# Suffix sums from a high and a low part, and steps of the second block moved up

## The chip, the core and the metric

The kernel is one program on one core of a Trainium2 chip. Its engines work side by side, each through its own list of instructions in order: TensorE (PE, the matrix products; its weight loads are listed apart as PEld), VectorE (DVE), ScalarE (ACT), GpSimd (POOL), and SyncE (SP), which here issues the transfers of weights. They meet at semaphores. The metric is the device time of one launch in microseconds (us), lower is better; it was 1090.6 us before the change, the median of 3 runs.

## The reference

Input is x of 256 tokens by 1024 features, all in float32. A first block of two layers (a mixer of mLSTM, block-sparse and native sparse attention, then a feed-forward part) is followed by a second block of two layers that mixes three kinds of attention. Cut to what matters here:

```python
def first_block(x, ...):
    for l in range(DEPTH):                                   # 2 layers
        h = rmsnorm(x, norm_mix[l])
        proj = jnp.einsum('bsd,de->bse', h, w_in[l])
        ...                                                  # y_m, y_b, y_n
        mix = jnp.concatenate([y_m, y_b, y_n], axis=-1)
        x = x + jnp.einsum('bse,ed->bsd', mix, w_out[l])
        h = rmsnorm(x, norm_ffn[l])
        u = jnp.square(jax.nn.relu(jnp.einsum('bsd,df->bsf', h, w_ff1[l])))
        x = x + jnp.einsum('bsf,fd->bsd', u, w_ff2[l])

def stick_breaking_attention(q, k, v):                       # 8 heads of 64
    for i in range(2):                                       # queries in blocks of 128
        z = jnp.einsum('bhqd,bhkd->bhqk', q[:, :, q0:q1], k[:, :, :q1]) * scale
        strict = pos[:q1][None, :] < pos[q0:q1][:, None]
        log_keep = jnp.where(strict, jax.nn.log_sigmoid(-z), 0.0)
        log_rest = lax.cumsum(log_keep, axis=3, reverse=True) - log_keep
        a = jnp.where(strict, jnp.exp(jax.nn.log_sigmoid(z) + log_rest), 0.0)
        outs.append(jnp.einsum('bhqk,bhkd->bhqd', a, v[:, :, :q1]))

def hybrid_layer(x, w_in, ..., w_out, g_pre, g_post, ...):   # second block, 2 layers
    h = rms_norm(x, g_pre)
    p = h @ w_in
    qa, ka, va, ga, qs, ks, vs, gs, qf, kf, vf, gf, ff = jnp.split(p, split_at, axis=-1)
    ya = diff_attention(qa, ka, va, ...) * jax.nn.silu(ga)
    yb = stick_breaking_attention(qs, ks, vs) * jax.nn.silu(gs)
    yc = forgetting_attention(qf, kf, vf, cum_log_f) * jax.nn.silu(gf)
    y = jnp.concatenate([ya, yb, yc], axis=-1) @ w_out
    return x + rms_norm(y, g_post)
```

The second block's output has the shape of x, and it is the only output.

## The kernel before

**Weights.** All weights are streamed from memory in units of 128 x 1024 float32 (512 KB). SyncE issues a unit's transfer into one of four `raw` slots. ScalarE rounds it to `w_hi` (L1405, type fp32r), VectorE takes the rest as `w_lo` (L1824), and a product of float32 accuracy is three fp32r matmuls, high by high, high by low, low by high (`exact_product`, L852 to L854; in the first feed-forward product, ff1, L918 and L920). Activations are kept in such parts too (`h_parts`, `mixT_hi`, `mixT_lo`). ScalarE and VectorE split weights ahead of need: before a step that reads a bank, `split_to` issues the splits of the units up to AHEAD = 3 in front of it. So a split stands in each engine's list between the other steps, and what stands behind it waits for it.

**Order.** One list of steps is written at the start by Python loops; each engine then issues its share in that order. In the second block `side2(p)` puts the attention's steps at position p, which is behind the p-th unit of the layer's projections. For a stick-breaking head the stages are Z (PE: scores; ScalarE: abs, exp, log of one plus it, L1669), K (VectorE, L2323: adds max(z, 0), so that `softp` holds the softplus of the score), R (PE, L1333 to L1335: suffix sums of `softp`, added to the scores that are still in the bank; ScalarE then takes the exponential) and V (PE: values). Heads go in pairs, four pairs a layer, every third position. `softp` is 128 x 384 for a head: queries 0 to 127 see 128 keys, queries 128 to 255 see 256.

**Suffix sums.** R multiplies by two constants of 128 x 128, a triangle (`C_RTRI`) and a matrix of one value (`C_NONES`). Both and `softp` are plain float32, which PE takes in two passes. The rest of the layer's PE work beside them is the projections, 256 columns at a time, and the heads' products.

**Gates and the mix.** `gate_silu` (ScalarE, L1650) takes the silu of the gates and loads that function's table for it and another one behind it. `mix_full` (VectorE, L2310) multiplies attention output in a bank by the gate, for four pairs of heads' columns n = 0 to 3; `mix_hi` (ScalarE) and `mix_lo` (VectorE, L2316) split the product. The forgetting heads ("fox") have the stages S (PE: scores; VectorE: row maxima, L1910 and L1913; ScalarE: exps, L1442 and L1444), N (VectorE: reciprocals of the sums, L1923 and L1924; GpSimd: scaling, L1720), T (PE: transposes, L1061, into bank 6; ScalarE: copy `probsT`, L1448) and V (PE: L1038, into bank 7).

**Banks.** PE's results go into eight banks of PSUM. `use(key, bank)` names the bank of a step; the PE opens it only when the reader of the bank's last content has freed it. The first feed-forward product has passes t = 0, 1, ...; each has four groups c of results, all in banks 4 to 7, which VectorE reduces (L2201) before the next pass opens them. The second feed-forward product (ff2) then opens banks 0 to 3 for four sums.

**Ends of the first block's layers.** The output projection ends in a "tail", whose last three features f = 1, 2, 3 wait for the transposed mix (`mix_turn`, two of them). Norm factors are a diagonal matrix (`factor_diag`, L1885), which a product (L1114) turns into a row.

## Time and profile before

| what | value |
| --- | --- |
| median of 3 runs | 1090.6 us (1089.24 to 1091.53) |
| profiled execution | 1088.39 us, its span 1086.6 us |
| granted TensorE clock, mean | 0.997 |
| PE busy | 1064.1 us, 98% of the span |
| DVE busy / ACT busy / POOL busy | 741.4 / 618.6 / 80.8 us |
| DMA | 179.04 MB, 165 GB/s mean |
| chain that ended last | PE 79%, DVE 8%, ACT 6%, issue 4%, DMA 3% |

All engines' times come from one profiled execution. Busy time counts an instruction from start to end; matmuls are pipelined, so a matmul's duration is longer than the distance to the next one's start, and that distance is what a matmul costs in a stream. "Idle before" is the time in which the engine had nothing in work ahead of an instruction, with what ended it.

### The profile page before, as it was taken

What the parts mean: (1) busy time and instruction counts of PE and PEld (TensorE: products, weight loads), DVE (VectorE), ACT (ScalarE), POOL (GpSimd) and SP (SyncE); (2) the same over time, 40 slices, a digit from 0 to 9 for tenths busy, and PEclk for the clock granted to TensorE, in tenths of its full rate; (3) what the DMA queues carried; (4) which work ended last, traced back from release to release, by engine and by line L of the source; (5) the groups of instructions that cost most, each with busy time, mean ns of one, the idle gap of its engine ahead of it and who ended that gap; (6) DMA issues with size and microseconds to landing.
All of it is one profiled execution on the core that took longest, in us unless ns stands there. A gap on an engine that the chain in (4) does not pass through costs nothing.

```text
span 1086.6 us, 16764 instructions
## 1 busy us (share of the span) xinstructions
PE 1064.1 (98%) x6396; PEld 908.1 (84%) x6396; DVE 741.4 (68%) x1296; ACT 618.6 (57%) x1039; POOL 80.8 (7%) x96
## 2 busy tenths in 40 slices
PE   8999999999999999999999999999999999999997
PEld 7898888888888988888888887898987778989876
DVE  5889777677667888787766675684465657844554
ACT  6776754344436768563444354855656548556562
POOL 1010110000000100110000000004011000040120
PEclk9999999999999999999999999999999999999999
DMA  9853365555657534446566654654444456544432
GB/s 320 268 153 118 99 189 182 190 173 187 211 183 216 168 112 133 123 151 208 162 207 198 191 160 147 197 156 136 120 150 136 136 156 194 156 131 123 155 118 76
DMA packets 89404, 179.04 MB, mean 165 GB/s; under 512 B 8989, under 2 KB 20637, under 8 KB 89325
## 3 DMA queue, kind: packets, MB, share of 16 engines
q1 hardware_dynamic: 88605, 176.58, 52.1%
q10 hardware_dynamic: 720, 1.40, 0.4%
q8 instruction: 51, 0.84, 0.3%
q14 instruction: 28, 0.23, 0.1%
HBM read 176.90 MB, written 1.05 MB: 164 GB/s over the span
## 4 chain that ended last, share of the span: by engine, by line
PE 79%; DVE 8%; ACT 6%; issue 4%; DMA 3%; SPq 0%; DVEq 0%; POOL 0%; ACTq 0%; POOLq 0%
PE bank L852 18%; PE bank L854 17%; PE bank L853 17%; PE bank L918 11%; PE bank L920 5%; DVE w_lo L1824 2%; DMA raw<-in_w_in 2%; PE bank L1004 2%; ACT w_hi L1405 2%; PE bank L953 2%; PE bank L1061 1%; PE bank L1038 1%; DVE vecs L1833 1%; PE bank L1027 1%; PE bank L1333 1%
## 5 line engine op out<-in xcount | busy, mean ns | idle before, releaser
L1824 DVE TENSOR_TENSOR w_lo<-raw,w_hi 128x1024 fp32r<-128x1024 f32 (+1 forms) x319 | 385.7, 1221 | 228.1 <-ACT w_hi L1405 225.4
L1405 ACT ACTIVATE w_hi<-raw 128x1024 fp32r<-128x1024 f32 (+1 forms) x319 | 330.7, 1052 | 181.9 <-PE bank L854 96.7
L918 PE MATMUL bank<-h_parts,w_hi 128*128 128x512 f32 x512 | 180.7, 396 | 1.0 <-DVE arena L2201 0.7
L852 PE MATMUL bank<-h_parts,w_hi 128*128 128x256 f32 x512 | 149.3, 292 | 0.0
L853 PE MATMUL bank<-h_parts,w_hi 128*128 128x256 f32 x512 | 144.7, 283 | 0.0
L854 PE MATMUL bank<-h_parts,w_lo 128*128 128x256 f32 x512 | 144.6, 282 | 0.0
L852 PE MATMUL bank<-w_hi,h_parts 128*128 128x512 f32 (+1 forms) x352 | 141.2, 401 | 3.2 <-DVE w_lo L1866 2.0
L920 PE MATMUL bank<-h_parts,w_lo 128*128 128x256 f32 x512 | 143.4, 280 | 0.0
L853 PE MATMUL bank<-w_lo,h_parts 128*128 128x512 f32 (+1 forms) x352 | 136.5, 388 | 0.0
L854 PE MATMUL bank<-w_hi,h_parts 128*128 128x512 f32 (+1 forms) x352 | 136.5, 388 | 0.0
L918 PEld LDWEIGHTS bank<-h_parts,w_hi 128*128 128x128 f32 x512 | 96.0, 188 | 24.8 <-issue 2.6
L852 PEld LDWEIGHTS bank<-h_parts,w_hi 128*128 128x128 f32 x512 | 97.8, 191 | 4.7 <-issue 3.5
L852 PE MATMUL bank<-w_hi,u_hi 128*128 128x512 f32 x256 | 101.0, 395 | 0.0
L854 PE MATMUL bank<-w_hi,u_lo 128*128 128x512 f32 x256 | 100.0, 391 | 0.0
L853 PE MATMUL bank<-w_lo,u_hi 128*128 128x512 f32 x256 | 100.0, 391 | 0.0
L853 PEld LDWEIGHTS bank<-h_parts,w_hi 128*128 128x128 f32 x512 | 98.0, 191 | 0.1
L854 PEld LDWEIGHTS bank<-h_parts,w_lo 128*128 128x128 f32 x512 | 97.8, 191 | 0.0
L920 PEld LDWEIGHTS bank<-h_parts,w_lo 128*128 128x128 f32 x512 | 96.7, 189 | 0.5
L852 PEld LDWEIGHTS bank<-w_hi,h_parts 128*128 128x128 f32 x352 | 66.5, 189 | 19.0 <-issue 4.3
L854 PEld LDWEIGHTS bank<-w_hi,h_parts 128*128 128x128 f32 x352 | 66.5, 189 | 13.3
L853 PEld LDWEIGHTS bank<-w_lo,h_parts 128*128 128x128 f32 x352 | 66.7, 189 | 11.2
L852 PE MATMUL bank<-w_hi,mixT_hi 128*128 128x512 f32 x160 | 65.3, 408 | 1.2 <-DVE mixT_lo L1843 1.2
(295 smaller groups left out, 1523.3 us busy)
## 6 DMA issues: line engine op xcount, KB each, us to landing
raw<-in_w_in SPq DMA_DIRECT2D x143, 512.0 KB, 3.8
raw<-in_w_ff SPq DMA_DIRECT2D x128, 512.0 KB, 4.3
raw<-in_w_out SPq DMA_DIRECT2D x40, 512.0 KB, 3.4
raw<-in_w_in SPq DMA_DIRECT2D x8, 404.0 KB, 5.5
xn<-in_cmp_w SPq DMA_DIRECT2D x8, 256.0 KB, 5.4
x_sb<-in_x SPq DMA_DIRECT2D x2, 512.0 KB, 9.1
mix<-in_cmp_w SPq DMA_DIRECT2D x4, 256.0 KB, 4.0
gain<-in_cmp_w SPq DMA_DIRECT2D x4, 256.0 KB, 5.6
```

The costliest lines, as they stand in the source:

```text
L852: pe.matmul(out_ap, s_hi, m_hi, start=start, stop=False, **kw)
L853: pe.matmul(out_ap, s_hi, m_lo, start=False, stop=False, **kw)
L854: return pe.matmul(out_ap, s_lo, m_hi, start=False, stop=stop, **kw)
L918: pe.matmul(ps[:, :].rearrange("p (a t) -> p a t", a=2), hi[:, kk, f], h_parts[:, :, k, :], start=k == 0, stop=False, skip_group_check=True)
L920: mm = pe.matmul(ps[:, 0:T], lo[:, kk, f], h_hi[:, k, :], start=False, stop=k == KD - 1, skip_group_check=True)
L953: mm = pe.transpose(ps[:, n * P:(n + 1) * P], src[:, i, k * P:(k + 1) * P], ident)
L1004: mm = pe.matmul(ps[c][:, lo:lo + cols], q[:, i * P:(i + 1) * P], k[:, 0:cols], start=i == 0, stop=i == 1 and last == "scores", skip_group ...
L1027: pe.matmul(ps[c][:, lo:lo + T - i * P], k, q, start=i == 0, stop=False, skip_group_check=True)
L1038: mm = pe.matmul(ps[HD * c:HD * c + HD, lo + b * P:lo + T], values_of[c](b), weights_of[c][:, b * T:T + b * P], start=first and b == 0, st ...
L1061: mm = pe.transpose(ps[:, b * P:(b + 1) * P], probs[:, h % 3, b * P:(b + 1) * P], ident)
L1405: act.activation(slot(w_hi, u), slot(raw, u), ACT.Copy).then_inc(hi_ready, 1)
L1824: dve.tensor_tensor(slot(w_lo, u), slot(raw, u), slot(w_hi, u).bitcast(F32), ALU.subtract)\
```

## The change

1. R: VectorE splits `softp` into `keep_hi` and `keep_lo` behind K (a cast and a difference, 128 x 384 each, for 16 heads), and PE multiplies each by an fp32r copy of the triangle, `after`, in one matmul of 384 columns. The product with the matrix of one value stays as it is. PE waits for the new semaphore `keep_split`. `after` is filled once, by a cast beside the loading of the feed-forward constants.
2. K stands at lag 0, behind Z of both heads of its pair, before at lag 1.
3. `gate_silu` stands first at positions 33 and 48, before behind the heads' steps there. `mix_full` stands last at 33, 38, 48 and 52 (before 34, 38, 49, 52), `mix_hi` at 36, 39, 50, 53 (before 35, 39, 50, 53), and `mix_lo` one position behind it.
4. The norm's diagonal, `r_diag`, is made at position 4, its product `r_row` stays at 5.
5. ff1 uses banks 0, 1, 2, 4 in its first pass and 5, 6, 7, 3 in the second; the norm's transposes always use 4 to 7.
6. The tail of the first block's output projection waits for one `mix_turn` at its start and for the other ahead of f = 2.

```diff
--- before.py
+++ after.py
@@ -140,7 +140,7 @@
     def norm_turn(n, i, u):
-        use(("norm", n, i, u), 2 * i if n in FFN_NORMS and u else 4 + 2 * u + i)
+        use(("norm", n, i, u), 4 + 2 * u + i)
         step("norm", n, i, u)
@@ -369,7 +369,7 @@
             for c in range(4):
-                use(("ff1", l, t, c), 4 + c)
+                use(("ff1", l, t, c), ((0, 1, 2, 4), (5, 6, 7, 3))[t][c] if t < 2 else 4 + c)
             for q in range(4):
@@ -414,6 +414,13 @@
         def side2(p):
+            if p in (33, 48):
+                step("gate_silu", l, p // 48)
+            for n, turn_at in enumerate((36, 39, 50, 53)):
+                if p == turn_at:
+                    step("mix_hi", l, n)
+                if p == turn_at + 1:
+                    step("mix_lo", l, n)
             for name, first, sp, groups_of in ((("diff", l), 12, 1.5, 2), (("fox", l), 41, 1.25, 4)):
@@ -421,12 +428,14 @@
                             head_steps(name, h, stage, groups_of)
-            for stage, lag in (("V", 3), ("R", 2), ("K", 1), ("Z", 0)):
+            for stage, lag in (("V", 3), ("R", 2), ("Z", 0), ("K", 0)):
                 for h in range(stage == "V", 8, 2 if stage == "V" else 1):
...
                 step("stats", 4 + l)
+            if p == 4:
+                step("r_diag", 4 + l)
             if p == 5:
@@ -440,12 +449,8 @@
                     single(i, "mix_turn", 1, l, 0, i)
-            if p in (33, 48):
-                step("gate_silu", l, p // 48)
-            for n, full_at in enumerate((34, 38, 49, 52)):
-                for c, part_of in enumerate(("mix_full", "mix_hi", "mix_lo")):
-                    if p == full_at + c:
-                        step(part_of, l, n)
+            if p in (33, 38, 48, 52):
+                step("mix_full", l, (33, 38, 48, 52).index(p))
 
@@ -505,6 +510,7 @@
         masks = sb("masks", [P, 2 * P], BF16)
+        after = sb("after", [P, P], F32R)
         x_sb = sb("x_sb", [P, NT, D])
@@ -623,6 +629,7 @@
 
+        keep_hi, keep_lo = (exact(f"keep_{n}", vecs_at, at_col, 2, 384) for n, at_col in (("hi", 0), ("lo", 768)))
         post_gain = vecs[:, 1536:1536 + D]
@@ -680,7 +687,7 @@
         lam_dots, lam_exp = sem("lam_dots"), sem("lam_exp")
-        stick_log = sem("stick_log")
+        stick_log, keep_split = sem("stick_log"), sem("keep_split")
         y_sumsq, y_ms, y_rstd = sem("y_sumsq"), sem("y_ms"), sem("y_rstd")
@@ -932,9 +939,11 @@
 
-            def tail_products(name, a, features, turned_inside=()):
+            def tail_products(name, a, features, turned_inside=(), second_half=None):
 
                 for n, (f, hi_f, lo_f) in enumerate(features):
+                    if f == second_half:
+                        drained(pe, ("mix_turn", 0, name[2], 1))
                     if n < len(turned_inside):
@@ -1270,8 +1279,9 @@
                     elif kind == "tail" and s[1] == "out":
-                        drained(pe, ("mix_turn", 0, l, 1))
-                        tail_products(("out", 0, l), s[-1], [(f, mixT1_hi[0][:, f, :], mixT1_lo[0][:, f, :]) for f in (1, 2, 3)])
+                        drained(pe, ("mix_turn", 0, l, 0))
+                        tail_products(("out", 0, l), s[-1], [(f, mixT1_hi[0][:, f, :], mixT1_lo[0][:, f, :]) for f in (1, 2, 3)],
+                                      second_half=2)
                     elif kind == "tail":
@@ -1328,10 +1338,10 @@
                         ps = open_bank(("stick", l, "R", h))
-                        keep = softp[:, h % 2, :]
-                        after, every = const[:, C_RTRI:C_RTRI + P], const[:, C_NONES:C_NONES + P]
-                        pe.matmul(ps[:, 0:T], after, keep[:, 0:T], start=False, stop=False, skip_group_check=True)
-                        pe.matmul(ps[:, T:T + P], after, keep[:, T:T + P], start=False, stop=False, skip_group_check=True)
+                        pe.wait_ge(keep_split, 8 * l + h + 1)
+                        keep, every = softp[:, h % 2, :], const[:, C_NONES:C_NONES + P]
+                        for part_of in (keep_hi, keep_lo):
+                            pe.matmul(ps[:, 0:384], after[:, :], part_of[:, h % 2, :], start=False, stop=False, skip_group_check=True)
                         close(pe.matmul(ps[:, P:T], every, keep[:, T:T + P], start=False, stop=False, skip_group_check=True), s)
@@ -1990,6 +2000,7 @@
                             link(dve.tensor_copy(masks[:, n * P:(n + 1) * P], const[:, c:c + P]))
+                        link(dve.tensor_copy(after[:, :], const[:, C_RTRI:C_RTRI + P]))
                         dve.wait_ge(second_loaded, 16 * SECOND_LOADS)
@@ -2242,7 +2253,7 @@
                         norm_step(*s[1:])
-                    elif kind == "r_row":
+                    elif kind == "r_diag":
                         factor_diag(s[1])
@@ -2321,6 +2332,9 @@
                         free(dve.scalar_tensor_tensor(softp[:, h % 2, :], ps[:, 0:384], 0.0, softp[:, h % 2, :], ALU.max, ALU.add), z)
+                        link(dve.tensor_copy(keep_hi[:, h % 2, :], softp[:, h % 2, :]))
+                        dve.tensor_tensor(keep_lo[:, h % 2, :], softp[:, h % 2, :], keep_hi[:, h % 2, :].bitcast(F32), ALU.subtract)\
+                            .then_inc(keep_split, 1)
                     elif kind == "mix_turn":
...
                         turned(s, mixT_hi[g][:, 0:4, t], mixT_lo[g][:, 0:4, t])
```

VectorE's list at the first pair of stick-breaking heads of layer 3 of 4 (the first of the second block), before. `w_lo` is the low part of a weight unit, `vecs` holds `softp`:

```order
L1824 TENSOR_TENSOR w_lo<-raw,w_hi 128x1024 [waits hi_ready] x2
L2323 SCALAR_TENSOR_TENSOR vecs<-bank,vecs 128x384 [waits stick_log,bank_filled4]
L2323 SCALAR_TENSOR_TENSOR vecs<-bank,vecs 128x384 [waits stick_log,bank_filled5,bank_freed4]
L1824 TENSOR_TENSOR w_lo<-raw,w_hi 128x1024 [waits hi_ready,bank_freed5]
L1824 TENSOR_TENSOR w_lo<-raw,w_hi 128x1024 [waits hi_ready] x2
L2323 SCALAR_TENSOR_TENSOR vecs<-bank,vecs 128x384 [waits stick_log,bank_filled4]
```

The same place in the changed kernel, where `keep_hi` and `keep_lo` are the parts of `softp`:

```order
L1834 TENSOR_TENSOR w_lo<-raw,w_hi 128x1024 [waits hi_ready]
L2334 SCALAR_TENSOR_TENSOR vecs<-bank,vecs 128x384 [waits stick_log,bank_filled4]
L2335 CAST keep_hi<-vecs 128x384 [waits bank_freed4]
L2336 TENSOR_TENSOR keep_lo<-vecs,keep_hi 128x384 [waits vector_step]
L2334 SCALAR_TENSOR_TENSOR vecs<-bank,vecs 128x384 [waits stick_log,bank_filled5]
L2335 CAST keep_hi<-vecs 128x384 [waits bank_freed5]
L2336 TENSOR_TENSOR keep_lo<-vecs,keep_hi 128x384 [waits vector_step]
L1834 TENSOR_TENSOR w_lo<-raw,w_hi 128x1024 [waits hi_ready] x3
```

Both K steps stand one `w_lo` earlier, each with two more instructions behind it.

PE's list there, from the last projection matmul before R to the first behind it, before and then now (`const` holds the two matrices):

```order
L854 MATMUL bank<-h_parts,w_lo 128x256
L1333 MATMUL bank<-vecs,const 128x256 [waits bank_freed4]
L1334 MATMUL bank<-vecs,const 128x128
L1335 MATMUL bank<-vecs,const 128x128
L1333 MATMUL bank<-vecs,const 128x256 [waits bank_freed5]
L1334 MATMUL bank<-vecs,const 128x128
L1335 MATMUL bank<-vecs,const 128x128
L852 MATMUL bank<-h_parts,w_hi 128x256 [waits lo_ready_vector]
```

```order
L861 MATMUL bank<-h_parts,w_lo 128x256
L1344 MATMUL bank<-keep_hi,after 128x384 [waits keep_split,bank_freed4]
L1344 MATMUL bank<-keep_lo,after 128x384
L1345 MATMUL bank<-vecs,const 128x128
L1344 MATMUL bank<-keep_hi,after 128x384 [waits keep_split,bank_freed5]
L1344 MATMUL bank<-keep_lo,after 128x384
L1345 MATMUL bank<-vecs,const 128x128
L859 MATMUL bank<-h_parts,w_hi 128x256 [waits lo_ready_vector]
```

The matmuls stand at the same place; PE now waits for `keep_split` ahead of each head.

VectorE's list at forgetting heads 4 to 7 of the same layer, before and then now. The 128x512 `mix` row is `mix_full` for n = 2:

```order
L1913 ISA probs,small<-bank,const 128x256 [waits vector_step]
L1913 ISA small 128x1
L1824 TENSOR_TENSOR w_lo<-raw,w_hi 128x1024 [waits hi_ready,bank_freed5]
L1923 RECIPROCAL small<-small 128x2x2 [waits exp_ready]
L1924 RECIPROCAL small<-small 128x2 [waits vector_step]
L2310 TENSOR_TENSOR mix<-bank,arena 128x512 [waits gate_ready,bank_filled7]
L1824 TENSOR_TENSOR w_lo<-raw,w_hi 128x1024 [waits hi_ready,bank_freed7]
```

```order
L1923 ISA probs,small<-bank,const 128x256 [waits vector_step]
L1923 ISA small 128x1
L2321 TENSOR_TENSOR mix<-bank,arena 128x512 [waits gate_ready,bank_filled7,bank_freed5]
L1834 TENSOR_TENSOR w_lo<-raw,w_hi 128x1024 [waits hi_ready,bank_freed7]
L1933 RECIPROCAL small<-small 128x2x2 [waits exp_ready]
L1934 RECIPROCAL small<-small 128x2 [waits vector_step]
L1834 TENSOR_TENSOR w_lo<-raw,w_hi 128x1024 [waits hi_ready] x2
```

The row `mix` now stands ahead of a `w_lo` and of the two reciprocals, which wait for ScalarE's exponentials.

## Rows read from the trace of the kernel before

**Rows 1.** Page, parts 1 and 2: busy us (share) xinstructions, and tenths in 40 slices.

```profile
PE 1064.1 (98%) x6396; PEld 908.1 (84%) x6396; DVE 741.4 (68%) x1296; ACT 618.6 (57%) x1039; POOL 80.8 (7%) x96
...
PEclk9999999999999999999999999999999999999999
```

**Rows 2.** Waits of PE, then PEld: line <- releaser: us in total, times, longest.

```profile
PE bank L1038 <- DVE mix L2310: 4.4, 4, 2.0
...
PE bank L918 <- DVE arena L2201: 0.7, 2, 0.3
...
PE bank L1114 <- DVE arena L1885: 0.5, 2, 0.3
...
PEld bank L1333 <- DVE vecs L2323: 3.2, 8, 0.8
```

**Rows 3.** Timeline, PE, first suffix sum: start us, us, engine line op tiles xcount [idle before].

```profile
743.79 0.28 PE L853 MATMUL bank<-h_parts,w_hi 128*128 128x256 f32 x1
743.91 0.28 PE L854 MATMUL bank<-h_parts,w_lo 128*128 128x256 f32 x1
...
744.92 0.39 PE L1334 MATMUL bank<-vecs,const 128*128 128x128 f32 x2
745.14 0.39 PE L1335 MATMUL bank<-vecs,const 128*128 128x128 f32 x2
```

**Rows 4.** Timeline, PEld (weight loads), first and last pair of the stick part.

```profile
744.38 0.30 PEld L1333 LDWEIGHTS bank<-vecs,const 128*128 128x128 f32 x2 [0.40 <-DVE vecs L2323]
...
746.13 0.19 PEld L852 LDWEIGHTS bank<-h_parts,w_hi 128*128 128x128 f32 x1
...
783.30 0.19 PEld L1333 LDWEIGHTS bank<-vecs,const 128*128 128x128 f32 x1 [0.80 <-DVE vecs L2323]
```

**Rows 5.** Timeline, DVE, before the first suffix sum.

```profile
742.56 1.30 DVE L1824 TENSOR_TENSOR w_lo<-raw,w_hi 128x1024 fp32r<-128x1024 f32 x1 [5.28 <-ACT w_hi L1405]
743.79 1.14 DVE L2323 SCALAR_TENSOR_TENSOR vecs<-bank,vecs 128x384 f32<-128x384 f32 x2
```

**Rows 6.** Timeline, ACT, before the first suffix sum.

```profile
741.05 0.52 ACT L1669 ACTIVATE vecs<-vecs 128x384 f32<-128x384 f32 x1
741.48 1.04 ACT L1405 ACTIVATE w_hi<-raw 128x1024 fp32r<-128x1024 f32 x1
```

**Rows 7.** Groups by line and form, DVE: xcount | busy us, mean ns | idle us.

```profile
L2050 DVE COPY vecs<-vecs 128x512 f32<-128x512 f32 x2 | 0.9, 426 | 0.1
```

**Rows 8.** Timeline, all engines, forgetting heads 4 to 7.

```profile
826.09 1.28 ACT L1650 ACT_TABLE_LOAD   x1
...
829.43 0.49 PE L1061 MATMUL bank<-const,probs 128*128 128x128 f32 x3
...
830.82 0.47 ACT L1448 ACTIVATE probsT<-bank 128x384 f32<-128x384 f32 x1
...
833.51 0.18 DVE L1923 RECIPROCAL small<-small 128x4 f32<-128x4 f32 x1 [1.27 <-ACT probs L1444]
...
833.80 0.69 DVE L2310 TENSOR_TENSOR mix<-bank,arena 128x512 f32<-128x512 f32 x1
833.97 2.60 POOL L1720 TENSOR_TENSOR probs<-probs,small 128x384 f32<-128x384 f32 x2 [8.38 <-DVE small L1924]
...
834.64 0.87 PE L1038 MATMUL bank<-probsT,arena 128*64 128x256 f32 x8 [1.96 <-DVE mix L2310]
```

**Rows 9.** Timeline, DVE and PE, second pass of the first FFN product.

```profile
171.62 2.86 DVE L2201 TENSOR_REDUCE arena<-bank 128x256 f32<-128x512 f32 x4
...
171.95 0.40 PE L852 MATMUL bank<-w_hi,u_hi 128*128 128x512 f32 x1
...
174.02 0.39 PE L852 MATMUL bank<-w_hi,u_hi 128*128 128x512 f32 x1
```

**Rows 10.** Timeline, DVE, ahead of the first output projection's tail.

```profile
136.14 0.68 DVE L1843 TENSOR_TENSOR mixT_lo<-bank,mixT_hi 128x512 fp32r<-128x512 f32 x1
```

## The prediction made before the run

> **What bounds the kernel now.** First the page's busy times and clock: PE is busy 98% of the span, and the granted clock is full in all 40 slices [rows 1]. There is no cheaper engine to hide behind and no clock to win back: the time changes only where PE's own work changes, or where one of its few gaps opens or closes. Next PE's waits, which list those gaps; the change touches three lines by moving what they wait for: L1038, 4.4 us in four waits for `mix_full`, L1114, 0.5 us for the diagonal, and L918, 0.7 us for a bank [rows 2]. For L1333, the first matmul of a suffix sum, the weight loads' list is the better one, since it counts from the end of the last load: 3.2 us, 8 times [rows 2]. Then the timeline around these, to see what stands in front of the late instruction.
>
> **How a matmul is priced.** By the distance of starts, not by its duration. Two fp32r matmuls of 256 columns start 0.12 us apart though each is shown 0.28 long, and a float32 matmul of 128 columns is two records in 0.22 us, L1334 to L1335 [rows 3], so 0.11 a record, half as many columns per ns; one of 256 columns is then twice that, 0.43 a matmul. At 2.4 columns per ns (the full clock of [rows 1] is the higher level, 2.4 GHz) 256 columns are 0.107 us, so a matmul adds 0.013; 384 columns are then 0.160 + 0.013, about 0.175 us.
>
> The Trainium skill's "TensorE: Matmul & The Clock Gate", section "Back-to-back issue gap", gives a smaller cost beside the columns, 2.5 ns; by it a 384-column matmul would be 0.162 us and all the suffix sums together 0.4 us cheaper than I take. The trace's spacing is 0.12 for 256 columns where that rule has 0.109, so the row decides, and the sum goes by it.
>
> **R, the matmuls.** A pair of heads now has two fp32 products of 256 columns and four of 128, which is 2 x (0.43 + 0.22 + 0.22) = 1.74 us; the trace has 746.13 − 744.38 = 1.75 from its first load to the next product's [rows 4]. After: four fp32r matmuls of 384 columns and two fp32 ones of 128, 4 x 0.175 + 2 x 0.22 = 1.14. Saved 0.61 a pair, 8 pairs in two layers: **−4.9 us**. The bounds: by durations a 384-column pass could be as long as 0.2 (−4.1), and at columns alone 0.16 (−5.3).
>
> **R, the entry.** The same rows show why R starts late. The last projection matmul is at 743.91 [rows 3], the loads have finished and stand idle for 0.40 until 744.38, for a K of VectorE [rows 4]. Both K are one group from 743.79, 1.14 long, behind a `w_lo` of 1.30 that started at 742.56 when `w_hi` was done; `w_hi` ran 741.48 to 742.52 [rows 5, 6]. The second head's log had been ready at 741.05 + 0.52 = 741.57 [rows 6]. So K was not waiting for its data but for the weight ahead of it in VectorE's list. In the new list each K stands ahead of that `w_lo`. What a head costs VectorE: K 0.57 (half of 1.14), the cast and the difference. A cast of 384 columns isn't in the trace; a float32 copy of 512 took 0.426 [rows 7], and no reason makes it free: between 0.2 (half of that) and 0.43, I take 0.36, since the copy's own row is the nearest. The difference of two 128x512 tiles took 0.69 [rows 8], for 384 columns some 0.55. Sum 1.5 a head. The second head's parts are there 1.5 behind its log, at 743.1; PE comes to R at 743.91 + 0.12 = 744.03. That leaves 0.9 us, so the wait should go, at the last pair too, whose 0.80 is the longest [rows 4]. Eight idle stretches sum to 3.2 [rows 2]; a load of 0.19 starts every 0.12, so each stretch hides 0.07 more of PE's time: **−3.7 us** for both layers. The other end is 0, if the parts come 0.9 later than I work out and a new wait stands where the old one did; beyond 3.7 there is nothing to gain, since no gap would be left.
>
> **What that does to VectorE's weights.** The two heads' six instructions, 3.0 us, now stand ahead of the second `w_lo`; VectorE begins them in the 5.28 us that it sits idle today [rows 5], at the second head's log (741.57) at the latest, so they end at 743.1 instead of that `w_lo` starting at 742.56: it is 0.5 to 0.8 later. In the trace it is done at 743.86 [rows 5]. A unit of projection is some 2.9 us of PE (24 matmuls of 0.12 [rows 3]) and splits run three units ahead, so PE needs it about 7 us later; VectorE is busy 68% of the span [rows 1]. Cost 0; if that cover were gone it is the fourth rival.
>
> **Mix and gates.** L1038 waits 4.4 us in four waits [rows 2]; two of them are 1.96 ahead of 834.64 and its like in the other layer, the other two sum to 4.4 − 3.9 = 0.5. There `mix_full` ran from 833.80 to 834.49, behind reciprocals that started at 833.51 after 1.27 of waiting for ScalarE's exps [rows 8]. The new list puts `mix_full` ahead of them, and PE would go on at 834.64 − 1.96 − 0.16 = 832.5 (0.16 is what PE loses behind a gap besides its idle time: a load of 0.19 and the refilling, less what overlaps). But then the next is late: the transposes of head 6, which PE reaches after the values' 0.87 [rows 8], at 833.4. They need ScalarE's exps, the reciprocals, and GpSimd's scaling. ScalarE's table load (1.28, from 826.09) and silus stand before head 5's copy now as then, only one copy further ahead, in time in which ScalarE waits for PE; so the copy, at 830.82 behind a `w_hi` today, can follow the transposes of 829.43 at 829.9 and end at 830.3. From the end of today's copy, 831.29, to the reciprocals at 833.51 are 2.2, from these to GpSimd's start at 833.97 0.46, and one head's scaling is half of 2.60 [rows 8]: 830.3 + 2.2 + 0.5 + 1.3 = 834.3. So a wait of 0.9, by the rounding of these steps 0.5 to 1.0, takes the place of 2.12: I take −1.3 a layer, **−2.6 us**; ends −1.1 and, if nothing is late next, −2.1 a layer. The early waits (0.25 each, 0.30 with the spacing) go too, for the silu of n = 0 is moved ahead of the heads' steps: **−0.6 us**, and at worst 0, if the exps of R, which that silu now stands in front of on ScalarE, come late by as much.
>
> **The diagonal.** L1114 waits 0.27 twice [rows 2], with the 0.16 of refilling behind it 0.43. Made one position, one unit (2.9 us), earlier, it can't be late: **−0.9 us**.
>
> **Banks of ff1.** The first pass closes 4 to 7; the second now opens 5, 6, 7 and 3, which nobody holds: 0.34 + 0.16 saved in each of two layers [rows 2]. But ff2 opens bank 3 as its fourth sum, at 174.02, ten matmuls behind 171.95, and VectorE's reduction of the last pass, 171.62 plus 2.86 for four, gives the last bank free at 174.48 [rows 9]. It waits 0.46 there, or 0.4 to 0.6 with the refilling. The two cancel: **0**, between −0.5 and +0.3 a layer.
>
> **The tail and the cast.** `mixT_lo` of the second `mix_turn` is done at 136.14 + 0.68 = 136.82 [rows 10], a microsecond before the tail is reached: its wait is never last, so moving it is worth 0. The cast into `after`, 0.2 us of VectorE once, where it holds PE already: **+0.2**.
>
> **Sum.** −4.9 − 3.7 − 2.6 − 0.6 − 0.9 + 0 + 0.2 = −12.5; I take 12.3, leaving 0.2 for 16 more switches between fp32r and fp32 (0.01 each: the 1.75 of the trace against records of 1.74). With every term at its small end the gain is 4.1 + 0 + 2.2 + 0 + 0.5 − 0.6 − 0.2 = 6.0, with every one at its large end 5.3 + 3.7 + 4.2 + 0.6 + 0.9 + 1.0 = 15.7. The profiled execution would be 1088.4 − 12.3 = 1076.1. It lies 2.2 us under the median of the runs, so on their basis 1090.6 − 12.3 = **1078.3 us**.
>
> **Rivals.**
>
> (a) The forecast, −9.5 to −14.5, 1076 to 1081: 0.68.
>
> (b) The hand-over is late. K, cast and difference make a chain of two heads; if ScalarE's logs come later in the other pairs (they share ScalarE with `w_hi`, 1.04 each [rows 6]) or an instruction is 0.3 longer than I take, the entry's 3.7 stays: −8.6, 1082.0. For it: at the last pair R waits 0.80 now [rows 4]. Against: 0.9 us of slack at the first. 0.14.
>
> (c) Switching costs. Each head goes from fp32r to fp32 and back inside R, at most by a matmul's duration beyond its spacing, 0.28 − 0.12 = 0.16, some 0.2 us, 16 times: +3.2, 1081.5. For it: nothing in the trace joins the two forms so often; against: 744.38 to 746.13 holds a switch at both ends and its records alone make 1.74. 0.06.
>
> (d) Nothing is late next at the forgetting heads: −1.6 more, 1076.7. For it: GpSimd sits idle 8.38 before its scaling [rows 8]. Against: the chain of copy, exps and scaling just worked out. 0.07.
>
> (e) Slower. `w_hi` of a unit depends on nothing new, but `w_lo` of it stands behind K, which waits for ScalarE's three activations. If VectorE's delay passes its lead of 7 us, PE starves for a unit at each pair: 8 x 2.9 = +23, less 12.3: 1101. From the point at which a K waits over 7 us. For it: VectorE's list is in order, and its steps wait longer than before; against: 5.28 idle [rows 5]. 0.04.
>
> (f) The loads don't overlap as priced. The Trainium skill's "TensorE: Matmul & The Clock Gate", section "The mechanism", has a weight load overlap a matmul in flight only where their row groups differ; here both use all 128 rows. The trace disagrees: loads of 0.19 follow matmuls 0.12 apart [rows 3, 4]. Taken as a mechanism of this kernel: a pair has 12 records before and 8 after; if each record paid 0.11 for its load besides its columns, 4 fewer in 8 pairs would be 3.5 us more gain, 1074.8. 0.01.
>
> That an edit does nothing (tail, banks) is part of the sum.
>
> **Range and chances.** The forecast's own range, 1076 to 1081, is that of the sum with two of its terms toward one end. Widened over (b), (c) and (d) it is 1075.5 to 1084.0, which leaves out (e), (f), and the tails of the sum's ends at 1074.9 and 1084.6. A measurement of this kernel can't tell 0.2%, 2.2 us, from no change. Faster by more, under 1088.4, is all but (e) and what isn't foreseen: 0.93; within it 0.03; slower 0.04.
>
> **What the profile of the changed kernel would show.** R of a pair 1.1 to 1.2 us from its first load to the next product's, and no PE wait for the difference that gives `keep_lo`: if a wait stands there, (b). Two 384-column matmuls 0.17 to 0.18 apart. L1038 without a wait for `mix_full`, and a wait of the transposes in the forgetting part of 0.5 to 1.0 in each layer. No wait for the diagonal, none for L2201 at ff1, one of 0.4 to 0.6 at ff2's fourth sum. A granted clock below the full level in any slice would make the sum worthless, since every term is a distance at 2.4 GHz; so would a PE wait for `w_lo` in the stick part.

## The result, and the profile after

The changed kernel takes 1079.24 us, the median of 4 runs (1078.86 to 1080.72), against 1091.07 for the kernel before, run again beside it (1089.24 to 1091.64): ratio 0.9897, 95% interval 0.9880 to 0.9914. That is 11.8 us faster, where 12.3 had been forecast, and it lies in the forecast's range of 1076 to 1081. The profiled execution took 1078.86 us, its span is 1076.7. From the page of the changed kernel, engines' busy times and the granted clock, beside [rows 1]:

```profile
PE 1058.3 (98%) x6364; PEld 902.9 (84%) x6364; DVE 762.1 (71%) x1329; ACT 618.2 (57%) x1039; POOL 77.8 (7%) x96
...
PEclk9999999999999999999999999999999999999999
```

PE still decides, with 32 fewer records. The mean clock was 0.998 against 0.997 before (a digit 9 stands for 90% or more). VectorE got 20.7 us of work, and most of it costs nothing. The waits of PE, in the columns of [rows 2]:

```profile
PE bank L859 <- DVE w_lo L1834: 2.2, 5, 1.0
...
PE bank L1070 <- POOL probs L1730: 1.1, 2, 0.5
PE bank L859 <- DVE arena L2212: 0.7, 2, 0.4
```

The waits of [rows 2] for `mix_full`, for the diagonal, and for the bank at ff1 are gone. In their place stand the two that were forecast: GpSimd's scaling at the forgetting heads, and VectorE's reduction at the fourth sum of ff2. The timeline of PE at the second pair of stick-breaking heads of layer 3:

```profile
757.64 0.28 PE L861 MATMUL bank<-h_parts,w_lo 128*128 128x256 f32 x1
757.76 0.34 PE L1344 MATMUL bank<-keep_hi,after 128*128 128x384 f32 x1
757.94 0.34 PE L1344 MATMUL bank<-keep_lo,after 128*128 128x384 f32 x1
758.12 0.38 PE L1345 MATMUL bank<-vecs,const 128*128 128x128 f32 x2
758.25 0.42 PE L1344 MATMUL bank<-keep_hi,after 128*128 128x384 f32 x1
...
758.83 0.36 PE L859 MATMUL bank<-h_parts,w_hi 128*128 128x256 f32 x1
```

Read the starts: 0.12 from the last projection matmul to R, so no stall where the weight loads of the four pairs sat idle for 0.40, 0.20, 0.20 and 0.80 before (the first and the last are in [rows 4]); 0.18 for a 384-column matmul; and 758.83 − 757.76 = 1.07 for the block, from the first matmul of R to the next product's first. The first pair of a layer is different. PE, and with it VectorE and GpSimd, same layer:

```profile
743.19 2.69 POOL L1798 TENSOR_TENSOR xn<-xn,sub_gain 128x512 f32<-128x512 f32 x2
743.26 0.56 DVE L2334 SCALAR_TENSOR_TENSOR vecs<-bank,vecs 128x384 f32<-128x384 f32 x1
...
743.85 0.86 DVE L2335 CAST keep_hi<-vecs 128x384 fp32r<-128x384 f32 x1
...
744.75 1.55 DVE L2336 TENSOR_TENSOR keep_lo<-vecs,keep_hi 128x384 fp32r<-128x384 f32 x1
...
745.59 0.34 PE L1344 MATMUL bank<-keep_hi,after 128*128 128x384 f32 x1
...
746.44 0.41 PE L1344 MATMUL bank<-keep_hi,after 128*128 128x384 f32 x1
...
747.01 0.36 PE L859 MATMUL bank<-h_parts,w_hi 128*128 128x256 f32 x1
```

The cast took 0.86 and the difference 1.55 us, where the second pair has 0.36 and 0.56. So PE got the second head's parts late, and the block is 747.01 − 745.59 = 1.42. No line of the waits shows this; the gap is only in the starts. At the forgetting heads, beside [rows 8]:

```profile
827.44 0.49 ACT L1458 ACTIVATE probsT<-bank 128x384 f32<-128x384 f32 x1 [1.99 <-PE bank L1070]
...
830.15 0.18 DVE L1933 RECIPROCAL small<-small 128x4 f32<-128x4 f32 x1 [2.45 <-ACT probs L1454]
...
830.61 2.60 POOL L1730 TENSOR_TENSOR probs<-probs,small 128x384 f32<-128x384 f32 x2 [7.53 <-DVE small L1934]
...
831.49 0.55 PE L1070 MATMUL bank<-const,probs 128*128 128x128 f32 x3 [0.54 <-POOL probs L1730]
```

This is the chain that the prediction had followed: copy, exps, reciprocals, GpSimd. And at ff2, beside [rows 9], the fourth sum waits for the last reduction:

```profile
172.51 2.14 DVE L2212 TENSOR_REDUCE arena<-bank 128x256 f32<-128x512 f32 x3
...
174.71 0.50 PE L859 MATMUL bank<-w_hi,u_hi 128*128 128x512 f32 x1 [0.35 <-DVE arena L2212]
```

**Where the time went.** Both executions' matmuls can be laid side by side, and the difference of their starts read wherever it steps. Per place, in us, both layers together: stick part with the early mix −8.2, forgetting heads −2.9, diagonal −1.1, banks +0.1, cast +0.2. The second block alone is −12.0. The first block is +2.1 in this pair of executions: 0.5 from its first 90 us, 1.2 in the passes of ff1, 0.3 by the banks and the cast. The profiled spans therefore differ by 9.9 and the medians by 11.8; run e12 below looks into that.

The 0.5 is the sum of larger steps either way, which differ from execution to execution: the same matmul, PE's 600th, starts between 88.2 and 90.5 us in the 14 traces of this case. One of these steps is the clock. [rows 1] shows a 9 there, but this window of the kernel before, behind a wait of PE of 1.98 us, has a mean clock of 0.58 (the figure behind the five engines; 1.2 GHz for 3.4 us), and the same window of the changed kernel has 1.00:

```profile
7.00:11.00 4.00, 3.39 (x8) 2.75 (x9) 3.81 (x7) 4.00 (x8) 0.00 (x0) 0.58 1.06 393
```

### The profile page after: what moved, and what is told of

Read it like the earlier page. It is cut to its first block, busy times and chain, and to the rows that moved or that the text cites. A ratio compares the mean times of both kernels' runs of the same rounds, so it can differ in the third digit from the quotient of the medians.

```text
span 1076.7 us, 16741 instructions
## 1 busy us (share of the span) xinstructions
PE 1058.3 (98%) x6364; PEld 902.9 (84%) x6364; DVE 762.1 (71%) x1329; ACT 618.2 (57%) x1039; POOL 77.8 (7%) x96
## 4 chain that ended last, share of the span: by engine, by line
PE 84%; DVE 7%; ACT 3%; issue 2%; DMA 2%; SPq 1%; POOL 0%; DVEq 0%; POOLq 0%; ACTq 0%
PE bank L859 19%; PE bank L861 19%; PE bank L860 18%; PE bank L925 11%; PE bank L927 5%; PE bank L1013 2%; DVE w_lo L1834 2%; DMA raw<-in_w_in 2%; PE bank L962 2%; PE bank L1070 1%; PE bank L1047 1%; PE bank L1089 1%; PE bank L1088 1%; PE bank L1036 1%; ACT w_hi L1415 1%
```

## The experiments

Each is the changed kernel with one edit, unless told otherwise. "In the stage" means the distance of starts of the same matmuls in two executions. Most of these effects are smaller than the spread of a kernel's runs (1.9 us here), but in the two layers of one trace they mostly come out within 0.1 us of each other.

### e1: the suffix sums in float32 again, the log sum stays early

```diff
-                        pe.wait_ge(keep_split, 8 * l + h + 1)
-                        for part_of in (keep_hi, keep_lo): ...
+                        pe.matmul(ps[:, 0:T], tri, keep[:, 0:T], ...)
+                        pe.matmul(ps[:, T:T + P], tri, keep[:, T:T + P], ...)
```

> Part 1 undone in the changed kernel: R as three float32 matmuls straight from softp, no keep parts; K stays at lag 0. Theory: the saving of R is in PE's passes alone, so the blocks go back from 1.07 us (1.42 in the first pair of a layer) to 1.78, the entry stays at 0.12 because K's place in VectorE's list gives it: + 6 x 0.71 + 2 x 0.36 = +5.0 us on the changed kernel's 1079.2, so 1084.2. Rival: the move of K and the split belong together, so without the split part of the entry stalls (3.7 us) returns too, 1086 to 1088; or the cast and the difference load VectorE so much that leaving them out gives back over 1 us, under 1083.5.

Measured: 1082.14 us, ratio to before 0.9925 (0.9903 to 0.9947). PE's timeline at the first pair:

```profile
744.69 0.60 PE L1343 MATMUL bank<-vecs,const 128*128 128x256 f32 x2
...
746.37 0.36 PE L859 MATMUL bank<-h_parts,w_hi 128*128 128x256 f32 x1
```

All eight blocks take 1.68 and all entries 0.12. So the stall is removed by K's place alone, and the passes are worth 1.68 − 1.07 = 0.61 a pair, the forecast number. The block of before, 1.78, held 0.10 of restart behind the stall, which I had counted with the entry. In the stage the edit costs 2.0 us in each layer, not 2.5: the expectation of +5.0 had wrongly taken those 0.10 in each of the eight pairs. The median is only 2.9 above the changed kernel's, and so is the profiled span; of the span's missing 1.1, 0.9 lies in front of the stick part of layer 3, in the first 90 us and the passes of ff1, which the edit doesn't touch. Of the change's 8.2 us in the stick part, 3.7 are K's place, 4.2 the new product (8 x 0.61 less 2 x 0.35), and 0.4 the early mix. The first rival (stalls back) is out. The second named a time under 1083.5, and 1082.14 is under it; but its mechanism is not what did it, since by the blocks 2.1 a layer was due and 2.0 came, so that at most 0.1 a layer is VectorE's lighter load.

### e2: the log sum behind a weight's low part again

```diff
-            for stage, lag in (("V", 3), ("R", 2), ("Z", 0), ("K", 0)):
+            for stage, lag in (("V", 3), ("R", 2), ("K", 1), ("Z", 0)):
```

> K put back to lag 1, behind a w_lo, in the changed kernel; all else is kept, the split too. Theory: where K stands decides the entry. K began at 743.79 in the kernel before; two heads of K, cast and difference, 1.5 each, end 3.0 later at 746.8, the first head's at 745.3, where PE comes at 744.03: 1.2 to 1.3 us of wait for the first head and, after its 0.57 of matmuls, 0.9 for the second, 2.1 to 2.3 a pair and 1.5 to 3 where GpSimd works beside it; 8 pairs: +16 to +20 us, 1095 to 1099, slower than before the change. Rival: the lists have enough slack, so that only the old stalls of 3.7 us come back: 1083.

Measured: 1106.55 us, ratio to before 1.0151 (1.0126 to 1.0176): slower than before the change by 1.5%, and by 27 us than the changed kernel. The direction is the theory's, the size beyond its range. The waits of PE, then the first pair's timeline, then three windows of PE's clock there (the figure behind the five engines):

```profile
PE bank L1344 <- DVE keep_lo L2336: 18.4, 15, 3.8
```

```profile
744.41 3.52 POOL L1798 TENSOR_TENSOR xn<-xn,sub_gain 128x512 f32<-128x512 f32 x2
...
748.19 2.58 DVE L2336 TENSOR_TENSOR keep_lo<-vecs,keep_hi 128x384 fp32r<-128x384 f32 x1
...
750.92 0.66 PE L1344 MATMUL bank<-keep_hi,after 128*128 128x384 f32 x1 [3.79 <-DVE keep_lo L2336]
```

```profile
738.00:746.00 8.00, 8.00 (x50) 6.65 (x50) 2.65 (x5) 4.45 (x8) 6.50 (x5) 1.00 0.45 133
746.00:751.00 5.00, 1.21 (x11) 1.04 (x9) 4.93 (x5) 1.78 (x3) 4.28 (x2) 0.93 0.33 105
751.00:760.00 9.00, 8.95 (x53) 8.07 (x53) 3.52 (x5) 2.04 (x3) 0.00 (x0) 0.66 0.37 117
```

Pairs 2 to 4 lose 2.2 each, as expected (entry +1.2, block +0.95). The first pair loses 5.1, since one difference takes 2.58 beside GpSimd, and PE sits idle for 3.79. Behind that pause the clock is granted at the lower level, 1.2 GHz, for part of 751 to 760 (mean 0.66), which costs some 1.6 more. Layer 4 has the same pause of 3.79; there the clock is low in 979 to 983 (mean 0.57) and again in 996 to 1000 (0.57). So the layers lose 13.2 and 13.6 us in the stage, and 1.5 more are a fall of the clock at the border between them. Beyond the expected 16 to 20 us are the 2.9 that each first pair loses more than the others, and these falls of the clock. Part 2 is no refinement of part 1: the split without it would have been a loss.

### e3: silu and mix at their old places

```diff
-            if p in (33, 48):
-                step("gate_silu", l, p // 48)        (ahead of the heads' steps; now behind them)
-            if p in (33, 38, 48, 52):
+            for n, full_at in enumerate((34, 38, 49, 52)):
```

> Part 3 undone: silu, mix_full, mix_hi and mix_lo at their places of before. Theory: the two waits of PE for mix_full come back (2.04 and 0.20 us a layer by distances of starts), the wait for GpSimd's scaling (0.60) goes: +1.64 a layer, +3.3 in all, span 1080.0; L1038's like waits 4.4 us in four for mix again. Rival: the wait for GpSimd stays beside the old one, since its chain is late anyway: +4.5.

Measured: 1083.08 us, span 1081.1. Its waits, and the first of them in the timeline:

```profile
PE bank L1044 <- DVE mix L2318: 6.0, 4, 2.0
```

```profile
772.57 1.23 DVE L1831 TENSOR_TENSOR w_lo<-raw,w_hi 128x1024 fp32r<-128x1024 f32 x1 [3.04 <-ACT w_hi L1412]
773.71 0.69 DVE L2318 TENSOR_TENSOR mix<-bank,arena 128x512 f32<-128x512 f32 x1
774.54 0.87 PE L1044 MATMUL bank<-probs,arena 128*64 128x256 f32 x8 [1.04 <-DVE mix L2318]
```

In the stage 2.4 a layer, 4.8 in all. The wait for GpSimd does go, as the theory has it, but the first wait is now 1.04 where it was 0.23 in the kernel before. It isn't VectorE's new work: VectorE sat idle for 3.04 ahead of the `w_lo` in front of `mix_full`, until ScalarE's `w_hi`, which stands behind the silu and its two table loads (767.71 to 771.46). That chain ends no sooner than before, while PE now reaches the values 0.8 earlier, 0.7 by the shorter block and 0.16 by the entry. So part 3 is worth more beside part 1 than alone, 4.8 and not the 3.3 that I took from the two traces.

### e4: GpSimd waits for the keep parts

```diff
                         pool.wait_ge(h_ms_ready, l + 1)
+                        pool.wait_ge(keep_split, 8 * (l + 1))
```

> One wait added: GpSimd begins the norm and gate of the diff heads (11 us of work) only when all eight heads' keep parts of the layer are made. In the changed kernel the cast and the difference of the second head of the first pair took 0.86 and 1.55 us, where they take 0.36 and 0.56 elsewhere, while GpSimd's elementwise work ran; and R's second head came 0.35 late. Theory: VectorE instructions with all operands in SBUF are slowed by GpSimd beside them; without it they take 0.36 and 0.56, the first pair's R block 1.07 like the others, -0.35 a layer, -0.7 us, span 1076.0. Rival: the place in the list or the ScalarE log makes the first pair late, then the durations fall or stay but the block stays 1.42; or the diff part is then late for the output projection, where it costs 1 us or more.

Measured: 1078.10 us (1077.13 to 1078.83), span 1075.0. The two instructions by tile, duration in ns least/median/most:

```profile
L2336 DVE CAST keep_hi<-vecs x16: 359/360/362, 741.3 to 990.7; 128x384 fp32r<-128x384 f32 x16
...
L2337 DVE TENSOR_TENSOR keep_lo<-vecs,keep_hi x16: 557/559/561, 741.7 to 991.1; 128x384 fp32r<-128x384 f32 x16
```

All 16 are equal now, all eight blocks take 1.07, and the stage gives 0.36 a layer. In the changed kernel the same rows have a most of 861 and 1551. GpSimd's work beside them is the cause, not the list nor ScalarE's log. The slowing isn't gone, it has moved: GpSimd now does this work from 779 to 791, and a `w_lo` at 789.39 takes 3.06 us beside it where others take 1.23. No PE wait follows from that.

### e5: bank 3 reduced first

```diff
-((0, 1, 2, 4), (5, 6, 7, 3))[t][c]
+((0, 1, 2, 4), (3, 5, 6, 7))[t][c]
```

> Second pass of ff1 in banks 3, 5, 6, 7 in place of 5, 6, 7, 3. Theory: the gain of the new banks at ff1 (0.58 and 0.55 us) is given back at the fourth sum of ff2 only because bank 3 is reduced last; reduced first it is free 2 us sooner, the wait for L2212 (0.7 in two) goes, and 0.63 us a layer is kept: -1.25, span 1075.5 (plus or minus 0.5 us of chance in the start of the kernel, so it is read in the stage: the step at the 10th matmul of ff2 falls from 0.63 to 0). Rival: the wait moves to the next pass of ff1, which opens bank 7 now freed last, and nothing is won.

Measured: 1078.21 us, one run; in the stage −0.66 and −0.59, and the line for L2212 is gone from the waits. The next pass of ff1 doesn't wait. The span, 1076.1, is only 0.6 below the changed kernel's since this execution lost 1.5 us at the border of layers 3 and 4, which the edit doesn't touch. Its clock there:

```profile
864.00:866.00 2.00, 2.00 (x7) 1.51 (x6) 1.93 (x6) 2.00 (x4) 0.04 (x1) 0.50 0.79 253
```

512-column matmuls start 0.43 apart, at the lower level, from 863.4 to 866.8. e10 has the same at the same place, the changed kernel not (1.00 there).

### e6: the last matmul of R split too

```diff
-close(pe.matmul(ps[:, P:T], every, keep[:, T:T + P], ...), s)
+for part_of in (keep_hi, keep_lo):
+    mm = pe.matmul(ps[:, P:T], every[:, :], part_of[:, h % 2, T:T + P], ...)
```

> R's last matmul, the matrix of one value, split too: two fp32r matmuls of 128 columns in place of one float32 matmul; no float32 pass is left in R. Theory: 128 columns cost 0.053 + 0.013 = 0.066 us, two 0.13 in place of 0.108 + 0.029 and 0.08 more for the switch back, 0.22: -0.09 a head, a block of about 0.98 in place of 1.07, -1.4 us in all, 1077.8. Rival: weight loads of 0.19 can't follow one another faster than the 0.12 seen in the streams, then a head costs 0.02 more than now and the block 1.1: +0.3 us, 1079.5.

Measured: 1079.09 us, no change. PE at the second pair:

```profile
757.30 0.22 PE L1346 MATMUL bank<-keep_hi,every 128*128 128x128 f32 x1
757.36 0.27 PE L1346 MATMUL bank<-keep_lo,every 128*128 128x128 f32 x1
757.47 0.39 PE L1344 MATMUL bank<-keep_hi,after 128*128 128x384 f32 x1
757.70 0.34 PE L1344 MATMUL bank<-keep_lo,after 128*128 128x384 f32 x1
```

The first 128-column matmul takes 0.06, the one behind it 0.11, and the next head's first 0.23 instead of 0.18. The weight loads there start at 757.31, 757.41 and 757.52: at this pace a matmul of 0.06 does not cover the load behind it, so the rival's reason fits, though no run tests it by itself. The block is 1.10, not 0.98. It reads 0.03 longer than in the changed kernel, but costs nothing: up to the second matmul behind R it is 1.271 in both kernels, and over a layer's stick part the two are within 0.03. In the changed kernel the float32 matmul's second record is followed after 0.03 and the matmul behind that comes 0.08 late; both together are the 0.11 of a record. So the 0.08 that the expectation had taken for a switch, to be saved, was part of the matmul's own price. The cast that fills the fp32r matrix costs 0.26 once.

### e7 and e12: why passes of ff1 differ

e7 is the kernel before with an unused tile, e12 the changed kernel word for word.

```diff
+        after = sb("after", [P, P], F32R)      (e7 only)
```

> The kernel before with one thing added: an unused SBUF tile of 512 bytes a partition where the changed kernel has the fp32r triangle, which shifts the addresses of what is behind it. Of the passes of ff1, 64 matmuls each, every second took 11.17 us and the others 10.98 in the kernel before, while all twelve took 11.18 in the changed kernel: 1.2 us more. Theory: the addresses do it; then here all twelve take 11.18, +1.2 us on the span of the kernel before. Rival: it isn't the addresses (the banks, the code's place, or how the passes lie against other engines' work); then the passes alternate as before, span 1086.6 within 0.5.

> The changed kernel, word for word, once more. The passes of ff1, 64 matmuls each, take 11.18 us or alternate between 10.98 and 11.17; which of the two differs from kernel to kernel and from layer to layer. Theory: it is chance of the execution, so another execution of the same kernel differs from the first, where all twelve took 11.18. Rival: it belongs to the program, then all twelve take 11.18 again.

Measured: e7 1090.33 us, e12 1078.74, one run each. In e7 the first layer's passes alternate (10.98, 11.17) and the second's all take 11.18; in e12 it is the first that has 11.18 and the second that alternates. First and last matmul of the same pass, changed kernel, then e12:

```profile
502.91 0.40 PE L925 MATMUL bank<-h_parts,w_hi 128*128 128x512 f32 x1
...
514.09 0.28 PE L927 MATMUL bank<-h_parts,w_lo 128*128 128x256 f32 x1
```

```profile
503.23 0.39 PE L925 MATMUL bank<-h_parts,w_hi 128*128 128x512 f32 x1
...
514.21 0.28 PE L927 MATMUL bank<-h_parts,w_lo 128*128 128x256 f32 x1
```

11.18 against 10.98 in the second layer with one and the same program: there it is chance of the execution, 0.6 us, and addresses aren't needed to explain it. The first layer is another matter. Its six passes all take 11.18 in all eight executions with the changed kernel's banks (changed kernel, e1 to e4, e6, e11, e12). With other banks in ff1 they alternate in five of six (before, e5, e7, e8, e10) and are constant in e9. So chance may not be all of it there: part 5 may cost 0.6 us in the first layer, and e5's edit win it back. No run separates the two.

### e8, e10, e9: versions that beat both

e10 has the edits of e4 and e5; e8 has e6's as well; e9 is e10 with head 6 of the forgetting heads scaled by VectorE:

```diff
+                    if kind == "fox" and h == 6:
+                        dve.wait_ge(inverse_ready[kind], 4 * l + 4)
+                        dve.tensor_tensor(blocks_of, blocks_of, dst[:, 0, :]..., ALU.mult).then_inc(weights_scaled["fox"], 1)
```

> The changed kernel with three edits: GpSimd waits for the keep parts, bank 3 first in ff1's second pass, and the matrix of one value split in R. Theory: the three places are apart, so the gains add: -0.7, -1.25 and -1.4 on 1079.2, 1075.8 us. Rival: only the first two hold (the split of the last matmul is bound by the weight loads): 1077.5.

> The changed kernel with GpSimd's wait and bank 3 first, R's last matmul left in float32. Theory: places apart, so the gains add, 0.37 a layer for the one and 0.6 a layer for the other: -2.0 on 1079.2, 1077.2 us, and 0.24 us less than with the split last matmul, whose blocks took 1.099 against 1.069. Rival: one of the two is given back later, over 1078.

> GpSimd's wait and bank 3 first as before, R as in the changed kernel, and for the forgetting heads 6 and 7 VectorE scales head 6 behind its reciprocals; GpSimd scales head 7 behind it. Theory: what PE waits for now at the transposes of head 6 is GpSimd's scaling, 1.3 us after the reciprocals end at 830.53 (start 0.1 later, end 831.5); VectorE's takes about 0.56 and ends at 831.1, PE is there at 830.96: of the 0.60 a layer 0.1 to 0.2 stays, -0.8 us against the same kernel without it. Rival: the w_lo that this pushes back (0.6 us) or head 7, scaled later, holds PE instead: 0.

| kernel | us, median (range) | ratio to before (95%) |
| --- | --- | --- |
| e8 | 1076.00 (1075.77 to 1077.11) | 0.9865 (0.9848 to 0.9881) |
| e10 | 1077.35 (1075.78 to 1078.79) | 0.9874 (0.9854 to 0.9894) |
| e9 | 1074.84 (1074.65 to 1075.79) | 0.9853 (0.9833 to 0.9874) |

e10 comes out at its expected 1077.2. e8 meets its expected 1075.8 too, but by luck: 1.4 of it was to come from the third edit, which e6 shows to give nothing, and the mechanism told there is the rival's, 1077.5. That e8's median is lower than e10's lies within e10's wide spread. In e9 VectorE and PE at head 6:

```profile
827.69 0.56 DVE L1942 TENSOR_TENSOR probs<-probs,small 128x384 f32<-128x384 f32 x1
...
828.30 0.55 PE L1070 MATMUL bank<-const,probs 128*128 128x128 f32 x3 [0.22 <-DVE probs L1942]
```

The wait is 0.22 instead of 0.54, 0.3 a layer in the stage, so 0.6 of the expected 0.8. Its median leads e10's by 2.5. The profiled spans differ by 4.0: 0.6 by the edit, 2.3 at the kernel's start and 1.6 by e10's lower clock at 863, less 0.5 from the passes of ff1 and other small steps. Whether the medians differ by chance in the same way is not settled.

### e11: diagonal and tail as before

```diff
-            if p == 4:
-                step("r_diag", 4 + l)
-                        drained(pe, ("mix_turn", 0, l, 0))
+                        drained(pe, ("mix_turn", 0, l, 1))
```

> Parts 4 and 6 undone in the changed kernel: the diagonal at position 5, the tail waits for the second transposed mix at its start. Theory: the diagonal's two waits of 0.27 for L1885's like come back at the second block's two norms, +0.55 a layer by distances of starts, and the tail's stage is the same within 0.05. Rival: the diagonal's wait doesn't come back since its w_lo is earlier now; or the tail loses 0.5.

Measured: 1078.62 us, one run, 0.6 under the changed kernel's median and 0.1 under e12; in the stage the two diagonals cost 0.52 and 0.5, the tail nothing, and the wait is back:

```profile
PE bank L1121 <- DVE arena L1892: 0.5, 2, 0.3
```

## Why the prediction was right

- **R's matmuls, −4.9.** 0.61 a pair by e1, so 4.9, less 0.35 in the first pair of each layer: −4.2. The full clock that the prediction read off [rows 1] holds where it is used, in the second block, but not at 7.7 us. The 384-column spacing was 0.178 against 0.175. The price rule of rows at 256 and 128 columns carried.
- **The entry, −3.7.** All entries are 0.12; by e1 the stalls and their restarts go with K's place alone. The slack for the second head, worked out as 0.9, was 0.9 in the second pair (parts done 756.84, PE there at 757.76) and gone in the first (parts done 746.30, PE there at 745.59). What failed there is the price of the cast and the difference, 0.36 and 0.55: exact when VectorE is undisturbed, and 0.86 and 1.55 beside GpSimd. Rival (b) was thus right for one head in eight, at a price of 0.35 a layer and not the whole entry.
- **VectorE's weights, 0.** PE waits 2.2 us for `w_lo`, 1.1 of it in the first 43 us of the kernel, which no moved step precedes, and none in the stick part. Rival (e), slower, was not met, and would not have come about as told, by a lead of 7 us used up: e2 shows that 1.2 us of lateness a pair is enough, since it is paid at R and not at the weights.
- **Forgetting heads, −2.6, early mix −0.6.** −2.9 and −0.4. The new wait was forecast at 0.5 to 1.0 and is 0.54 of idle, 0.60 in the stage. Rival (d), nothing late next, is out. e3 shows that the early mix is worth more than either trace tells alone.
- **Diagonal, −0.9:** −1.1. **Banks, 0:** +0.1, a gain of 0.58 and 0.55 given back as 0.63 and 0.64; e5 shows that the give-back was not needed. Whether the new banks also make the first layer's passes slower is open (e12). **Tail and cast, +0.2:** +0.2; e11 has the tail at 0.
- **Rival (c)**, 0.2 a switch: the switches cost next to nothing, since R of a pair with a switch at both ends adds 1.76 in e1 (1.88 up to the second matmul behind it, less that matmul's 0.12), where the records alone sum to 1.74, and e6, with no switch left, is no faster. **(f)**: no load rule shows in R at 384 columns. But e6 has a case where a load isn't hidden, 0.11 behind a matmul of 0.06.

The terms as measured in the stages sum to −11.9, beside −12.3 forecast and −11.8 in the medians. That it was met within 0.5 us owes something to luck: the term for R was 0.7 and that for the early mix 0.2 too good, and those for the forgetting heads and the diagonal 0.5 too poor.

## What to carry to other kernels

Where PE is busy 98% of the span, price an edit by distances of starts and look, for each stall, at what stands in front of the late instruction in its engine's list; often it isn't data. Take such a distance beyond the first matmul behind the place too, since a cost can show up one matmul later (e6). When work is added to that late instruction, move it up first: the same split ended 12 us below the kernel before with the move and some 16 above it without. And when a wait goes, follow the chain behind it to what is late next, since that is where the next edit lies (GpSimd's scaling, bank 3).

## What the hardware showed

- VectorE instructions with all operands in SBUF took longer beside GpSimd's TENSOR_TENSOR: the cast 0.86 us instead of 0.36, the difference 1.55 and 2.58 instead of 0.56, `w_lo` 3.06 instead of 1.23 (e4). K, which reads PSUM too, kept its 0.56 there.
- After a pause of PE of 3.8 us the clock was granted at 1.2 GHz for part of the next 9 us. At the border of two layers, with idle stretches of about 1.1 and 0.48 in every trace, it fell in three executions (e2, e5, e10) and stayed full in the other eleven. Each fall at the border cost about 1.5 us.
- The same passes of ff1 took 10.98 or 11.18 us in two executions of one program; what decides it is not known.
- A float32 matmul of 128 columns costs 0.22 us and two fp32r matmuls of 128 columns in its place cost as much (e6); 384 columns in two fp32r matmuls cost 0.36 where float32 takes 0.65 (e1: 0.22 + 0.215 for 256 columns, 0.22 for 128).
